# A three-layer transformer kernel on one core: stage changes worked per block of 128 tokens, and the loads and units of the start regrouped

## What is computed

```
layer 0: u = rms_norm(h, g_mix[0]);  h += mla_and_stick_breaking(u @ w_in) @ w_out
         u = rms_norm(h, g_ffn[0]);  h += (silu(u @ w_gate) * (u @ w_up)) @ w_down
layer 1: u = rms_norm(h, g_mix[1]);  h += chunk_band_attention(u @ w_qkv) @ w_out
         u = rms_norm(h, g_ffn[1]);  h += swiglu as above
h = rms_norm(h, g_final)
block 2: hn = rms_norm(h, ln_g); proj = hn @ w_in_2; five groups of attention heads, gates,
         h += merged @ w_out_2
```

## Time and profile before

| | |
|---|---|
| time, median of 3 runs (lowest to highest) | 1100.59 us (1099.68 to 1101.82) |
| span of the profiled execution | 1096.3 us |
| median time less that span | 4.3 us |
| PE busy | 1008.8 us, 92% |
| DVE, ACT busy | 641.2 us, 58%; 599.4 us, 55% |
| mean granted clock of PE | 0.976 |
| HBM read | 168.68 MB, mean 155 GB/s over the span |

### The profile page before, as it was taken

The page is one execution under the profiler, slowest core; times in us unless marked ns, Lnnn a source line. Parts: engine busy times, 40 slices in busy tenths (PEclk is TensorE's granted clock), DMA queues, the critical chain, the costliest instruction groups (busy, mean ns, idle before and its releaser), DMA issues.

```text
span 1096.3 us, 13515 instructions
## 1 busy us (share of the span) xinstructions
PE 1008.8 (92%) x5026; PEld 825.2 (75%) x5026; DVE 641.2 (58%) x811; ACT 599.4 (55%) x922; POOL 21.8 (2%) x21
## 2 busy tenths in 40 slices
PE   4977789999999998789999999899999998899998
PEld 3866567888887786577888887687787876788876
DVE  3357656655455546456555555767585665667654
ACT  5466545545445546445544545657566566765661
POOL 1000003000000000001000000000000000000000
PEclk8998899999999999899999999999999999999999
DMA  7422317555664453229566555354533433336550
GB/s 265 138 73 82 111 47 261 192 191 166 202 196 163 156 191 118 74 85 310 201 195 195 183 191 185 125 190 143 165 115 115 134 101 132 101 119 206 168 192 39
DMA packets 99405, 170.34 MB, mean 155 GB/s; under 512 B 3668, under 2 KB 52747, under 8 KB 99365
## 3 DMA queue, kind: packets, MB, share of 16 engines
q1 hardware_dynamic: 96704, 161.23, 44.4%
q0 software_dynamic: 2336, 8.47, 2.3%
q10 hardware_dynamic: 324, 0.10, 0.0%
HBM read 168.68 MB, written 1.11 MB: 155 GB/s over the span
## 4 chain that ended last, share of the span: by engine, by line
PE 83%; ACT 8%; DVE 6%; issue 2%; DMA 0%; ACTq 0%; DVEq 0%
PE acc L431 16%; PE acc L391 12%; PE acc L393 11%; PE acc L392 11%; PE pair_ps L393 7%; PE pair_ps L391 7%; PE pair_ps L392 7%; ACT logit L886 3%; PE turn_ps L505 2%; PE acc L482 2%; ACT w_hi L754 1%; PE turn_ps L449 1%; ACT uT_hi L785 1%; PE pair_ps L493 1%; PE pair_ps L492 1%
## 5 line engine op out<-in xcount | busy, mean ns | idle before, releaser
L1221 DVE TENSOR_TENSOR w_lo<-w_raw,w_hi 128x2048 fp32r<-128x2048 f32 (+3 forms) x156 | 351.5, 2256 | 165.1 <-ACT w_hi L754 165.0
L754 ACT ACTIVATE w_hi<-w_raw 128x2048 fp32r<-128x2048 f32 (+3 forms) x156 | 290.5, 1863 | 106.4 <-PE acc L393 61.2
L391 PE MATMUL acc<-w_hi,uT_hi 128*128 128x512 f32 (+3 forms) x564 | 224.6, 398 | 13.3 <-DVE w_lo L1221 6.4
L393 PE MATMUL acc<-w_hi,uT_lo 128*128 128x512 f32 (+3 forms) x564 | 217.7, 386 | 0.0
L392 PE MATMUL acc<-w_lo,uT_hi 128*128 128x512 f32 (+3 forms) x564 | 217.5, 386 | 0.0
L391 PEld LDWEIGHTS acc<-w_hi,uT_hi 128*128 128x128 f32 x564 | 107.9, 191 | 36.4 <-DVE w_lo L1221 9.2
L391 PE MATMUL pair_ps<-w_hi,uT_hi 128*128 128x512 f32 x320 | 126.5, 395 | 0.0
L393 PE MATMUL pair_ps<-w_hi,uT_lo 128*128 128x512 f32 x320 | 124.9, 390 | 0.0
L392 PE MATMUL pair_ps<-w_lo,uT_hi 128*128 128x512 f32 x320 | 124.6, 389 | 0.0
L393 PEld LDWEIGHTS acc<-w_hi,uT_lo 128*128 128x128 f32 x564 | 107.7, 191 | 21.3
L392 PEld LDWEIGHTS acc<-w_lo,uT_hi 128*128 128x128 f32 x564 | 108.1, 192 | 18.6
(11 more groups left out here) (207 smaller groups left out, 1121.0 us busy)
## 6 DMA issues: line engine op xcount, KB each, us to landing
w_raw<-in_w_in SPq DMA_DIRECT2D x50, 1024.0 KB
w_raw<-in_w_gate SPq DMA_DIRECT2D x44, 512.0 KB
w_raw<-in_w_up SPq DMA_DIRECT2D x44, 512.0 KB
w_raw<-in_w_down SPq DMA_DIRECT2D x22, 1024.0 KB
w_raw<-in_w_out SPq DMA_DIRECT2D x12, 1024.0 KB
w_raw<-in_w_qkv SPq DMA_DIRECT2D x12, 1024.0 KB
w_raw<-in_w_branch SPq DMA_DIRECT2D x6, 1024.0 KB
bias<-rel_rows POOLq DMA_DIRECT2D x5, 1024.0 KB, 10.3
```

Source lines behind the costliest of these rows:

```text
L391: mm(o, xh, wh[:, k, :], start=first and k == 0, stop=False)
L393: done = mm(o, xl, wh[:, k, :], start=False, stop=last and k == len(kts) - 1)
L754: activation(w_hi[:, slot, 0:width], w_raw[:, slot, 0:width], ACT.Copy).then_inc(hi_done, 1)
L1221: v.tensor_tensor(w_lo[:, slot, 0:width], w_raw[:, slot, 0:width], w_hi[:, slot, 0:width].bitcast(f32), ALU.subtract).then_inc(lo_done, 1)
```

## The change

Per block instead of per bank: PE turns block 0 in the middle of block 1's half of the last projection unit (behind 8 of its 12 matmuls), and block 1 behind block 0's half of the next stage's first unit. A bank now takes two k-tiles of one block (128 columns each), and the same four banks serve both blocks one after the other, so block 1's transposes wait until the low parts of block 0 are made. The sixteen wide roundings, eight on ACT and eight on DVE, become thirty-two of 128 columns, eight of each per block. ACT now does block 0's roundings first, then the squares of both blocks, then block 1's roundings. DVE does, in order: the add of block 0, block 0's low parts, the add of block 1, half of unit F+2's low part, block 1's low parts, the other half.

At the start the gains, the identity and `rel_bias` come packed from the host in one array, loaded by two DMAs. SP issues x's first block, 2 k-tiles of weights, x's second block, 2 k-tiles, 4 k-tiles, with no wait ahead of them. POOL holds the constants until x's second block is there. The first chunk is three units (2, 2 and 4 k-tiles), and ACT squares x behind the rounding of these.

Packing and loads (SP, POOL, ACT's issues):

```diff
             n = Ordinals()
-            for blk in range(TB):
-                sp.dma_start(h[:, blk, :], x[0].rearrange("(b p) c -> p b c", p=P)[:, blk, :]).then_inc(x_loaded, 16)
+            def load_x(blk):
+                sp.dma_start(h[:, blk, :], x[0].rearrange("(b p) c -> p b c", p=P)[:, blk, :])\
+                    .then_inc(x_loaded[blk], 16)
 
...
+            def first_units(w, cols, width):
+
+                load_x(0)
+                kt0 = 0
+                for i, m in enumerate(FIRST_UNITS):
+                    load([(view(m, width), rows(w, kt0, m, cols))])
+                    kt0 += m
+                    if i == 0:
+                        load_x(1)
 
...
 
-            sp.wait_ge(tables, TABLES)
-            for i in range(3):
+            first_units(w_in0, slice(672, 1184), 512)
+            for i in range(1, 3):
                 chunk_units(w_in0, KT, slice(672 + 512 * i, 1184 + 512 * i), 512)
             chunk_units(w_in0, KT, slice(0, 384), 384)
...
             pool.memset(eps[:, :], EPS).then_inc(eps_set, 1)
+            pool.wait_ge(x_loaded[1], 16)
             for dst, src in ((onehot[:, :], bucket_onehot), (dist_m, dist_mask),
...
+            act.dma_start(ident, tables_in[:, 0:P]).then_inc(tables, 16)
+            act.dma_start(flat_logit[0:GAIN_ROWS, 0:P + 32], tables_in[0:GAIN_ROWS, P:TABLE_COLS]).then_inc(tables, 16)
 
```

PE:

```diff
                 for k, kt in enumerate(kts):
-                    if n.fresh is not None and blk == 0 and kt % 2 == 0:
-                        pe.wait_ge(turned_lo, n.fresh + kt // 2 + 1)
+                    if n.fresh is not None and kt % 2 == 0:
+                        pe.wait_ge(turned_lo, n.fresh + 4 * blk + kt // 2 + 1)
                     xh, xl = x_hi[:, kt, tokens(blk)], x_lo[:, kt, tokens(blk)]
                     mm(o, xh, wh[:, k, :], start=first and k == 0, stop=False)
                     mm(o, xh, wl[:, k, :], start=False, stop=False)
                     done = mm(o, xl, wh[:, k, :], start=False, stop=last and k == len(kts) - 1)
-                if blk == 0 and kt == KT - 1:
+                if blk == 1 and kt == KT - 1:
                     n.fresh = None
                 return done
+
+            def turn_second():
+
+                if n.second is not None:
+                    turn_block(1, n.second)
+                    n.second = None
 
...
                 for blk in range(TB):
                     if between:
                         between(blk)
+                    if blk == 1:
+                        turn_second()
                     if first:
                         since(pe, acc_read, n.chunk * 2 + (blk - 1))
...
                     xh, xl = oT_hi[:, kt, tokens(blk)], oT_lo[:, kt, tokens(blk)]
                     for i, (xp, wp) in enumerate(((xh, wh), (xh, wl), (xl, wh))):
+                        if norm is not None and k == 1 and i == 1:
+                            turn_first(norm)
...
+            def turn_block(blk, banks):
+
+                if n.h == TB:
+                    pe.wait_ge(x_loaded[blk], 16)
+                else:
+                    pe.wait_ge(h_ready, n.h - 2 * TB + blk + 1)
+                if blk == 1:
+                    pe.wait_ge(turned_lo, n.fresh + 4)
+                for kt in range(KT):
+                    c0 = (kt % 2) * P
+                    done = transpose(banks[kt // 2][:, c0:c0 + P], h[:, blk, P * kt:P * kt + P], ident)
+                    if kt % 2:
+                        done.then_inc(turned, 1)
+
+            def turn_first(norm):
+
                 n.fresh = n.bank
-                n.bank = n.bank + 4
+                n.bank = n.bank + KT
                 n.h += TB
+                n.second = stream_banks[norm]
+                turn_block(0, n.second)
 
```

ACT:

```diff
+            def split_block(blk, norm):
+
+                banks = stream_banks[norm]
+                for k0 in range(0, KT, 2):
+                    act.wait_ge(turned, n.bank + 1)
+                    for k in (k0, k0 + 1):
+                        c = GAIN_COL[norm] + k
+                        done = activation(uT_hi[:, k, blk * P:blk * P + P], banks[k // 2][:, (k % 2) * P:(k % 2) * P + P],
+                                          ACT.Copy, scale=gain_T[:, c:c + 1])
                     done.then_inc(turned_hi, 1)
                     n.bank = n.bank + 1
 
             def stream_norm(norm, gains=None):
 
                 gains = norm if gains is None else gains
+                split_block(0, gains)
                 for blk in range(TB):
                     act.wait_ge(h_ready, n.h + blk + 1)
                     row_squares(norm, h, D, blk)
-                    if blk == 0:
-                        split_banks(uT_hi, 0, KT, stream_banks[gains], gains)
+                split_block(1, gains)
                 row_root(norm, D)
                 n.h += TB
...
+            def first_qkv():
+                scaled_by(MIX0)
+                copy_qkv(0)()
+
             act.wait_ge(eps_set, 1)
 
-            for blk in range(TB):
-                act.wait_ge(x_loaded, 16 * TB)
-                row_squares(MIX0, h, D, blk)
             act.wait_ge(tables_T, 1)
             activation(gain_T[:, :], acc[3][:, 0:GAIN_ROWS], ACT.Copy).then_inc(gains_set, 1)
             activation(tabT[:, :], acc[3][0:32, 64:104], ACT.Copy).then_inc(gains_set, 1)
             act.wait_ge(gains_set, 2)
-            split_banks(uT_hi, 0, KT, stream_banks[MIX0], MIX0)
-            round_unit(0)
+            split_block(0, MIX0)
+            round_unit(0, FIRST_UNITS[0] * 512)
+            split_block(1, MIX0)
+            round_unit(1, FIRST_UNITS[1] * 512)
+            slot_step(FIRST_UNITS[2] * 512)
+            for blk in range(TB):
+                row_squares(MIX0, h, D, blk)
             row_root(MIX0, D)
-            round_unit(1)
             for group, row in enumerate((0, 2, 2, 2, 4)):
                 done = activation(g_col[:, 2 * group:2 * group + 2], gain_T[:, QK_COL + row:QK_COL + row + 2], ACT.Copy)
             link(done)
             n.used = 0
-            scaled_by(MIX0)
-            project([copy_qkv(i) for i in range(3)], (UNIT,) * 4 + (1536, 1536))
+            project([first_qkv] + [copy_qkv(i) for i in range(1, 3)], (UNIT,) * 4 + (1536, 1536))
```

DVE (`split_block` has the form of ACT's, with `scalar_tensor_tensor` into `uT_lo`):

```diff
+            def split_unit_start(width, ahead=2):
 
                 slot = (n.slot + ahead) % RING
                 dve.wait_ge(hi_done, n.unit + (ahead + 1))
                 v.tensor_tensor(w_lo[:, slot, 0:width], w_raw[:, slot, 0:width],
-                                w_hi[:, slot, 0:width].bitcast(f32), ALU.subtract).then_inc(lo_done, 1)
+                                w_hi[:, slot, 0:width].bitcast(f32), ALU.subtract)
...
+            def add_block(blk):
+
+                for half in range(2):
+                    c = slice(512 * half, 512 * half + 512)
+                    done = v.tensor_tensor(h[:, blk, c], acc[2 * blk + half][:, :], h[:, blk, c], ALU.add)
+                done.then_inc(h_ready, 1)
+
...
+            def add_and_stream(norm):
+
+                n.proj += 1
+                dve.wait_ge(proj_done, n.proj)
+                add_block(0)
+                split_block(0, norm)
+                dve.wait_ge(unit_used, n.unit + 1)
+                add_block(1)
+                split_unit_start(UNIT // 2)
+                split_block(1, norm)
+                split_unit(start=UNIT // 2)
+                n.next_unit()
 
 
...
-                slot_step()
                 n.handed, n.bank, n.exps = n0 + NF, b0 + NF, e0 + NF
-                add_projection()
+                add_and_stream(following)
 
...
+            split_unit(0, FIRST_UNITS[0] * 512)
+            split_block(1, MIX0)
+            split_unit(1, FIRST_UNITS[1] * 512)
+            slot_step(FIRST_UNITS[2] * 512)
             row_scales(MIX0, D)
-            split_unit(1)
 
             def distance_rows():
                 dve.wait_ge(consts, CONSTS)
```

More of the change, by code:

```diff
@@ L164, in build_program @@
         latent_banks = [acc[2][:, :]] + acc_banks
-        x_loaded = sem("x_loaded")
+        x_loaded = [sem(f"x_loaded{blk}") for blk in range(TB)]
         tables = sem("tables")
@@ L418, in chunk, with first_chunk, proj_half @@
                     chunk_unit(x_hi, x_lo, range(x_kt + k0, x_kt + k0 + m), width, k0 == 0, k0 + m == nkt)
-            def proj_half(kts, blk, first, last, ahead=0):
+            def first_chunk(width):
+                k0 = 0
+                for m in FIRST_UNITS:
+                    chunk_unit(uT_hi, uT_lo, range(k0, k0 + m), width, k0 == 0, k0 + m == KT)
+                    k0 += m
+            def proj_half(kts, blk, first, last, ahead=0, norm=None):
                 slot = (n.slot + ahead) % RING
@@ L437, in proj_half, with proj_unit @@
                     n.next_unit()
-            def proj_unit(kts, first, last):
+            def proj_unit(kts, first, last, norm=None):
                 for blk in range(TB):
-                    proj_half(kts, blk, first, last)
```

(50 more changed lines are left out.)

171 lines of the change are left out of this document (83 added, 88 removed).

## The result

The changed kernel takes 1109.62 us (median of four runs, 1104.69 to 1114.66) against 1100.32 for the kernel before on the same chip: ratio 1.0083 [1.0061, 1.0105]. Forecast were 1098.2 and a range up to 1102.3. The change is slower, by 9.3 us in the median. The four runs spread over 10 us, so this difference is known to some 2.4 us either way. The profiled execution is the slowest of the four, so its trace shows more loss than the median: 16.6 us at the last matmul.

A forecast was written before the change was run, and what follows sets the result against it. TensorE, busy 1008.8 of 1096.3 us, was taken to set the pace. Start 4.1 plus three stage changes 0.6 less LN2 2.35 gave 2.35 us less, 1098.2 from 1100.59; own range 1096.5 to 1100, eight-in-ten 1094.5 to 1102.3.

The forecast's parts named there:

- three of the stage changes: Changes into FFN0, MIX1 and FFN1: block 1's first matmul at T+9.2 instead of T+9.5; 0.2 us gained each, 0.6 together.
- covered by 0.3: At those three changes: F+2's low part ends at T+11.7, and PE wants it at T+12.0.
- as before, and lands several us ahead of use: At the start: each next SP load waits for a low part and causes no delay.
- the start: Kernel start: tables land at 5.7, first weight matmul near 11.2, second chunk at 27.4 against 31.50; 4.1 us gained.
- if a weight load ended a wait of PE: Anywhere in the trace: one of the signs that would show the forecast wrong; no size given.
- LN2: Fourth stage change: double chain of row scales starts later, PE resumes 2.35 us later, idle stretch grows to 5 us.
- Which I leave unchanged: At LN2: the granted clock, already fallen to 0.50 for 3.2 us, was assumed to stay as before.
- 1: Start and all stage changes: 128-wide roundings cost 0.32 instead of 0.26 us, giving 1103; chance 0.12.
- 4: Start and stage changes: shorter hand-offs, narrow instructions near 0.20 us, giving 1094.7; chance 0.15.
- Rival 2: All four stage changes: clock falls after PE idles 1.7 us behind the second transposes; 6 us more, 1104; chance 0.05.
- Rival 3: Start: tables land at 6.4 or the clock stays lower; 1.9 us gained instead of 4.1, 1100.4; chance 0.15.

The follow-up runs named there:

- experiment 3: Changed kernel, with POOL's four window loads (4 MB) held back to units 80 to 89 of the second FFN: 1104.06 us, ratio 1.0033.
- experiment 7: Changed kernel, with POOL's addition to the band table cut into sixteen pieces: 1105.02 us, ratio 1.0044.
- Experiment 2: Kernel before, with only F+2's low part moved behind the low parts of the turned h: 1114.44 us, ratio 1.013.
- Experiment 8: Changed kernel with band table and window loads held (experiment 5), plus both table loads at the head of SP's queue, ahead of x: 1100.6 us, ratio 1.0007.
- experiments 10: Changed kernel with the old stage changes, tables at the head of SP's queue, no loads held, POOL's addition in sixteen pieces: 1097.36 us, ratio 0.9977.
- 12: Changed kernel with tables first on SP's queue, windows held, addition in pieces, and the old stage change at LN2 alone: 1096.13 us, ratio 0.9962.
- experiment 11: Changed kernel with tables first on SP's queue, windows held, addition in pieces, and the new stage change at LN2 too: 1100.8 us, ratio 1.0001.
- experiment 6: Kernel before, with only the band table load and the window loads on POOL held back: 1108.53 us, ratio 1.0072.
- 4: Changed kernel, with halves of F+2's low part made ahead of each block's low parts of h: 1106.28 us, ratio 1.0053.
- experiment 5: Changed kernel, with POOL's 2 MB band table load held until 31 units are used, and the window loads held too: 1104.79 us, ratio 1.0046.

## Why the prediction was wrong

*The step that failed* is in the paragraph on three of the stage changes, where F+2's low part is made at T+11.7 and called "covered by 0.3". That compares it with PE's need alone. I followed PE, ACT and DVE past the moved low part and past the later add, and not the two queues that they release: SP's next load and POOL's band load. What that costs stood in the sum at nothing, without a reason; the only words on SP's loads, "as before, and lands several us ahead of use", were said of the start. The runs show two losses in its place. Late by 10 us, the low part sends w_down's load behind POOL's 4 MB, and holding those back gives 5.5 us (experiment 3). Adding block 1 2.0 us later moves POOL's addition onto a low part that PE needs, and cutting it in pieces gives 4.3 us (experiment 7). In the changed kernel's trace the two places cost 4.6 and 3.9 us. Experiment 2, with the move alone, lost 7.7 us to the same addition by way of another low part, and nothing at the second FFN.

The amounts do not add up: 5.5, 4.3 and the start's 4.3 make 14.1, and all three repairs together bring 9.0 (ratio 1.0083 to 1.0001). Each is measured with the others in different states and is uncertain by 2 to 4 us, and the falls of the clock differ from run to run. My list of signs had "if a weight load ended a wait of PE"; it ended two of ACT, and PE waited behind those.

*The start*: wrong by its input alone. I took 4.5 us from loads that had only 1 MB of x beside them, and did not ask what the first weights, no longer held back, would do to the tables. 101 KB took 8.2 us behind them. Experiment 8 moves only that, and gets 4.3 where I had 4.1.

*Three stage changes*: mechanism right, sign right. Across each, the shift falls by 0.6 to 0.7 at block 1's first matmul, of which 0.5 to 0.6 stay, where I had 0.2: that matmul comes at T+8.84 in the first FFN, not T+9.2. Comparing experiments 10 and 12 (12 also has the windows held), the new changes are worth 1.2 us for three, below what can be told apart.

*LN2*: right in kind. The chain loses 2.1 us (2.35 said), with the gap of 4.7 us said as 5. "Which I leave unchanged" for the clock was wrong: it stays at half through all twelve matmuls behind the longer gap, another 1.2 us. So even with all three repairs (experiment 11) the change is at 1.0001, and not 2.35 us ahead.

*Rivals*: 1 and 4 fall, a narrow instruction costs 0.25. Rival 2 put the clock's fall in the gaps behind block 1's transposes; there, in 1.41 us of standing still, it stays at 1.00 (third window). It fell instead behind the waits of 2.0, 2.7 and 4.7 us, and at places that no rival named. Rival 3 came nearest for the start, with late tables, but at 6.4 and not at 9.41, and with 1.9 us gained where 0.3 was.

## What to carry to other kernels

When a step moves, ask what its semaphore releases on the DMA queues, and what else is about to go out there; here a load of 1 MB that left just behind 4 MB instead of ahead of them landed 10.2 us after its issue, and TensorE lost 4.6 us by it. A small table that everything waits for belongs at the head of the queue that would flood the engines, not on an idle one beside it. Put no long GpSimd instruction that reads SBUF beside VectorE work with two SBUF inputs that TensorE needs: cut it in pieces.

## What the runs showed of the hardware

A VectorE subtraction with both inputs in SBUF ends 2.15 us after a GpSimd addition that started ahead of it, however long the rest of that was: 196.46 after 194.31, 199.91 after 197.75, 263.37 after 261.22, 272.21 after 270.06, and 196.35 after 194.20 in experiment 2. VectorE operations that read PSUM beside the addition kept their 0.69 us (190.33 in the kernel after).

Two loads of 101 KB in all on an idle queue took 8.2 us while another queue moved 2.6 MB; at the head of that other queue they were there 3.8 us after the second's issue (1.19 to 5.03).

The length of a stop of PE did not decide whether its clock fell. Waits of 2.01, 2.72 and 2.86 us (200 and 538 after, 273 in experiment 6) were each followed by half clock and moved the shift by 3.9, 4.6 and 4.6 us. Waits of 1.93 and 2.09 us for the same oT_lo (experiments 3 and 4, near 199) kept full clock and cost 2.3 and 2.4; one of 1.31 us (264 in experiment 5) kept it too and cost 1.6. The windows behind the wait at the first FFN, after and in experiment 3:
```profile
200.56:205.56 5.00, 5.00 (x15) 3.98 (x16) 4.97 (x5) 1.99 (x2) 0.00 (x0) 0.66 0.88 282
```
```profile
199.53:204.53 5.00, 5.00 (x22) 4.11 (x23) 4.97 (x5) 2.08 (x2) 0.00 (x0) 1.00 0.87 276
```
What else decides it stays open.
